# The first unit's query, key scores and routing made head by head, with the order of the gathered rows unchanged

## The chip, the cores and the metric

The kernel runs on one core of one Trainium2 chip. The metric is the time of one execution in microseconds (us), measured on the device. Lower is better.

## What is computed

The reference is two transformer blocks over 256 tokens of width 1024. The change lies in the expert layer of the first block (`peer_ffn`), which picks 16 of 16,384 experts for each of 8 heads and each token, and needs one row of `u` and one of `v` for each:

```python
def token_block(xt):                       # 128 tokens
    q = (xt @ wq).reshape(128, 8, 2, 128)
    s = jnp.einsum('thcd,hckd->thck', q, sub_keys)
    top_s, top_i = lax.top_k(s, 16)        # per head, for each of two key sets
    cand = top_s[:, :, 0, :, None] + top_s[:, :, 1, None, :]
    best_s, best_c = lax.top_k(cand.reshape(128, 8, 256), 16)
    i1 = jnp.take_along_axis(top_i[:, :, 0], best_c // 16, axis=-1)
    i2 = jnp.take_along_axis(top_i[:, :, 1], best_c % 16, axis=-1)
    expert = i1 * 128 + i2
    w = jax.nn.softmax(best_s, axis=-1)
    act = jax.nn.gelu(jnp.einsum('thkd,td->thk', u[expert], xt))
    return jnp.einsum('thk,thkd->td', w * act, v[expert])
```

Before it come a norm, the mixers and the output projection `w_out`; behind it a gate (`ple`) and the whole second block.

## The kernel before, in words

Each engine runs its own program, written out in order; the engines meet through counting semaphores (`wait_ge`, `then_inc`). Nothing reorders the work: whatever stands behind a waiting instruction on its engine waits too.

The tokens are two tiles of 128. A *unit* is one tile and one pair of heads (`HPAIR` = 2), so there are 8 units: 0 to 3 for tile 0, 4 to 7 for tile 1. A unit needs 32 gathered *rows* of `u` and 32 of `v` (`UROWS`); each is one indirect DMA of 128 x 1024 floats (0.52 MB), issued by POOL (`gather_u` L2603, `gather_v` L2616), with 8 slots for each side (`GATHER_SLOTS`). A row of `u` goes into a slot when DVE has used the one before it there (`u_used`). POOL first issues the 32 rows of unit 0, then waits for the key scores of all units (`sk_done`), and from then on alternates rows of `u` of the next unit and rows of `v` of this one.

For unit 0 the work goes through the engines thus. PE makes the query (`tile_query`, L973: four blocks of 128 columns, two for each head, 8 matmuls each, in one PSUM bank). ACT copies it (`query`, L1434). PE makes the scores (`key_scores`, L995). ACT copies them (`scores_out`, L1440). DVE searches the 16 best of each key set (`best_keys`, with helper `best16`), adds them in pairs and searches the 16 best sums (`best_sums`, L2165 to L2175), turns the places into expert numbers (`places`, `route`, L2195 to L2213, two operations on 128 x 1024 and a reduction of as much) and signals `idx_ready`. The four steps handle both heads of the unit; only the searches are called for each head.

PE's order around it is: turn tile 0, query 0 and scores 0 (unit 0), turn the mixer output of tile 1, output product of tile 1 (`tile_out(1)`, L959, two halves), query and scores of unit 1, turn tile 1, queries and scores of units 4 and 5, then those of the other four.

ACT's order is: the roots of tile 1's two mixer norms (L1279), which wait for DVE, then the copies of query 0 and scores 0, the token copy for DVE's products (L1447), and the copies of the turned tile 1 (L1416), on which the output product of tile 1 waits.

DVE's order is: key search, sums, places and routes of unit 0, residual of tile 1 (L1773), its mean, the first product of unit 0 (`products(0, 0, 1)`, L2220), the norm of tile 1 (L1785), key search and sums of unit 1, seven more products of unit 0, places and routes of unit 1, and the rest of unit 0's products.

SP loads the weights in chunks of 2 MB into a ring of three slots (L525); a chunk's load is issued when the chunk that held its slot is done (`chunk_done`). Chunk 1 of `peer_wq`, for the query of unit 1, waits for the first half of the output product of tile 1; chunk 2 for the second half; chunk 3 for the query of unit 4.

## Time and profile before

| | us |
|---|---|
| three runs | 1649.35, 1650.64, 1655.22 |
| the profiled execution | 1648.42 |
| its span in the profile | 1646.6 |
| PE busy in the span | 1429.4 |
| DVE busy | 972.0 |
| ACT busy | 537.5 |
| POOL busy | 510.8 |

The three runs have the median 1650.64. The span is what the profiler saw between the first and the last instruction; the execution's own time is 1.8 us more. Busy times are sums over the whole span; the engines work beside one another, and a matmul's row covers its way through a pipeline, so a busy PE is not a PE at its peak. A row of the timeline gives the start, the busy time, the operation, and in brackets how long the engine sat idle before it and what ended that.

### The profile page before, as it was taken

Reading aid. Unit: us, or ns where it says so; the run is one execution under the profiler, and the core shown is the slowest. Engines: PE = TensorE matmul, PEld = TensorE weight load, DVE = VectorE, ACT = ScalarE, POOL = GpSimd, SP = SyncE. Lnnn points to the kernel's source line nnn. Section 1 sums busy time; section 2 is a strip of 40 time slices with the busy share of each in tenths; the row PEclk is TensorE's granted clock in tenths of the full one; section 3 lists DMA queues with packets and bytes.
Section 4 is the critical chain, followed back from the end, with each engine's and each line's share of the span. In section 5 each row is a group of like instructions: output and inputs, shape, how many; then the busy total and the mean of one; then the engine's idle time right before and its main releaser. Section 6 shows DMA issues by size and latency. Waiting matters only on the chain. (4 is left out here: it accounts for less than half of the span.)

```text
span 1646.6 us, 17356 instructions
## 1 busy us (share of the span) xinstructions
PE 1429.4 (87%) x6624; PEld 943.0 (57%) x6624; DVE 972.0 (59%) x1758; ACT 537.5 (33%) x807; POOL 510.8 (31%) x550
## 2 busy tenths in 40 slices
PE   7999989677777777777777789999999989999998
PEld 6665667222222222222222466668998778689986
DVE  2255488566666667666545643565775365657763
ACT  3253321212121111111113245643443354434432
POOL 4000025767777777777676200000000000000000
PEclk9899999999999999999999999999999999999999
DMA  9323069999999999999999334224553545345543
GB/s 307 119 102 115 3 257 391 404 409 410 409 409 409 409 409 409 409 409 409 410 409 372 134 140 153 102 81 136 193 180 128 195 158 185 104 136 172 180 149 133
DMA packets 162578, 413.75 MB, mean 251 GB/s; under 512 B 11337, under 2 KB 57659, under 8 KB 162368
## 3 DMA queue, kind: packets, MB, share of 16 engines
q0 software_dynamic: 75632, 272.63, 42.1%
q1 hardware_dynamic: 86544, 138.58, 24.7%
q10 hardware_dynamic: 320, 1.43, 0.2%
q8 instruction: 53, 0.87, 0.2%
q14 instruction: 29, 0.24, 0.0%
HBM read 411.55 MB, written 1.05 MB: 251 GB/s over the span
## 5 line engine op out<-in xcount | busy, mean ns | idle before, releaser
L2220 DVE SCALAR_TENSOR_TENSOR arena<-arena,ps 128x1024 f32<-128x1024 f32 x256 | 309.3, 1220 | 224.0 <-DMA arena<-in_peer_u,routes 222.9
L2603 POOL DMA_INDIRECT arena<-in_peer_u,routes x256 | 241.8, 945 | 139.1 <-issue 63.2
L1813 DVE TENSOR_TENSOR w_lo<-ring,w_hi 128x2048 fp32r<-128x2048 f32 x66 | 151.1, 2292 | 103.3 <-ACT w_hi L1653 103.3
L1548 ACT ACTIVATE state<-cst,gatew 128x128 f32<-128x128 f32 x240 | 90.6, 397 | 342.9 <-PE ps L1047 342.8
L1653 ACT ACTIVATE w_hi<-ring 128x2048 fp32r<-128x2048 f32 x66 | 126.3, 1916 | 180.2 <-PE ps L1187 88.3
L1047 PE MATMUL ps<-mixed,state 128*128 128x512 f32 x240 | 118.5, 617 | 39.8 <-ACT state L1548 35.5
L1047 PE MATMUL ps<-wX,state 128*128 128x512 f32 x240 | 117.3, 611 | 40.9 <-DMA wX<-in_peer_v,routes 21.1
L1047 PE MATMUL ps<-xT,state 128*128 128x512 f32 x240 | 117.3, 611 | 39.0 <-ACT state L1548 26.5
L1047 PE MATMUL ps<-proj,state 128*128 128x512 f32 x240 | 117.3, 611 | 37.7 <-DMA proj<-in_peer_v,routes 20.2
L1047 PEld LDWEIGHTS ps<-mixed,state 128*128 128x128 f32 x240 | 41.5, 192 | 116.7 <-ACT state L1548 72.9
L1047 PEld LDWEIGHTS ps<-wX,state 128*128 128x128 f32 x240 | 40.6, 189 | 117.6 <-issue 71.4
L1047 PEld LDWEIGHTS ps<-xT,state 128*128 128x128 f32 x240 | 40.6, 189 | 115.6 <-ACT state L1548 67.4
L1047 PEld LDWEIGHTS ps<-proj,state 128*128 128x128 f32 x240 | 40.6, 189 | 114.3 <-issue 72.2
L1187 PE MATMUL ps<-x_lo,w_hi 128*128 128x256 f32 x704 | 99.4, 284 | 3.8 <-DVE x_lo L2458 3.8
L1187 PE MATMUL ps<-x_hi,w_hi 128*128 128x256 f32 x704 | 100.3, 285 | 0.0
L1187 PE MATMUL ps<-x_hi,w_lo 128*128 128x256 f32 x704 | 99.6, 284 | 0.0
L1187 PEld LDWEIGHTS ps<-x_lo,w_hi 128*128 128x128 f32 x704 | 91.3, 193 | 4.2 <-DVE x_lo L2458 4.2
L1187 PEld LDWEIGHTS ps<-x_hi,w_hi 128*128 128x128 f32 x704 | 91.4, 193 | 0.6 <-DVE x_hi L1794 0.4
L1187 PEld LDWEIGHTS ps<-x_hi,w_lo 128*128 128x128 f32 x704 | 91.6, 193 | 0.0
L2616 POOL DMA_INDIRECT proj<-in_peer_v,routes x64 | 62.7, 980 | 22.1 <-issue 16.8
L2616 POOL DMA_INDIRECT xT<-in_peer_v,routes x64 | 62.2, 971 | 20.1 <-issue 17.7
L2616 POOL DMA_INDIRECT wX<-in_peer_v,routes x64 | 61.0, 953 | 22.2 <-issue 16.5
(449 smaller groups left out, 2323.5 us busy)
## 6 DMA issues: line engine op xcount, KB each, us to landing
ring<-in_ffn_w_up SPq DMA_DIRECT2D x22, 2048.0 KB, 8.7
ring<-in_ffn_w_down SPq DMA_DIRECT2D x22, 1024.0 KB, 4.8
ring<-in_even_w_in SPq DMA_DIRECT2D x7, 2048.0 KB, 7.7
ring<-in_w_in SPq DMA_DIRECT2D x6, 2048.0 KB, 11.5
ring<-in_odd_w_in SPq DMA_DIRECT2D x6, 2048.0 KB, 7.7
ring<-in_peer_wq SPq DMA_DIRECT2D x4, 2048.0 KB, 8.7
ring<-in_w_out SPq DMA_DIRECT2D x2, 2048.0 KB, 7.9
arena<-in_peer_u,routes POOLq DMA_INDIRECT x256, 12.6
```

The lines of the kernel that those rows point to most:

```text
L1047: last = mm(ps[:, 4 + 2 * (u // PAIR_UNITS) + half_, :], diags[n % DIAGS], v_slots[b % GATHER_SLOTS][:, 512 * half_:512 * half_ + 512], st ...
L1187: last = mm(o, w[:, k, f * P:(f + 1) * P], x_[:, k, :], start=(step == k == 0), stop=(step == 2 and k == KD - 1))
L1548: do(diags[n % DIAGS], ident, ACT.Copy, scale=gatew[:, u * UROWS + b:u * UROWS + b + 1]).then_inc(diag_ready, 1)
L1653: do(w_hi[j % 2][:], w, ACT.Copy).then_inc(hi_ready, 1)
L1813: v.tensor_tensor(w_lo[j % 2][:], w, w_hi[j % 2][:].bitcast(F32), ALU.subtract).then_inc(lo_ready, 1)
L2220: v.scalar_tensor_tensor(row, row, 1.0, token_tile(u // PAIR_UNITS), ALU.mult, ALU.mult, accum_out=dots[:, b:b + 1]).then_inc(u_used, 1)
L2603: pool.indirect_dma_start(arena[:, b % GATHER_SLOTS, :], None, a["peer_u"][0], route_of(u, b))\
L2616: pool.indirect_dma_start(v_slots[b % GATHER_SLOTS], None, a["peer_v"][0], route_of(u, b))\
```

## The change

Unit 0's chain is split by heads. PE writes head 0's query into bank 2 and head 1's into bank 3 and signals each (`first_query`); the scores of a head (`head_scores`) go into banks 4 and 5, and those of head 0 stand inside the query of head 1, after 20 of the 32 matmuls. ACT copies a head's query and a head's scores by turns. DVE's `places` and `route` take a range of heads and are called for each head of unit 0, so that `idx_ready` counts up after head 0 and again after head 1; POOL waits for the first before row 0 and for the second before row 16. The order of the rows is the same. All other waits on `q_done`, `q_read`, `sk_done`, `sk_read` and `idx_ready` count one more; of them the diff shows those of `key_scores` and `scores_out`.

```diff
@@ -403,6 +403,14 @@
         def unit_scores(u):
 
             return proj[:, 2048 + 512 * u:2048 + 512 * (u + 1)]
+
+        def scores_count(u):
+
+            return SK_ORDER.index(u) + 2
+
+        def routed(u):
+
+            return u + 2
 
         def scores_at(u):
 
@@ -962,13 +970,38 @@
                         if (c, k) in steps:
                             attention_step(steps[c, k])
 
+            def head_scores(hd):
+
+                pe.wait_ge(q_read, hd + 1)
+                pe.wait_ge(keysT_ready, 1)
+                q_ = grid(proj[:, 0:1024], 2 * HPAIR, T)
+                for hc in (2 * hd, 2 * hd + 1):
+                    last = mm(ps[:, 4 + hd, hc * P:(hc + 1) * P], q_[:, hc, 0:P], keysT[:, hc, :], start=True, stop=True)
+                last.then_inc(sk_done, 1)
+
+            def first_query():
+
+                i1 = CHUNK_AT["peer_wq"]
+                begin(i1)
+                for j in range(2 * HPAIR):
+                    for k in range(KD):
+                        if j == 0:
+                            tile_ready("peer", 0, k)
+                        last = mm(ps[:, 2 + j // 2, j * P:(j + 1) * P], product_slot(i1)[:, k, j * P:(j + 1) * P], xT[:, k, 0:P],
+                                  start=(k == 0), stop=(k == KD - 1))
+                        if j % 2 and k == KD - 1:
+                            last.then_inc(q_done, 1)
+                        if (j, k) == (2, KD // 2 - 1):
+                            head_scores(0)
+                head_scores(1)
+
             def tile_query(c, tt, bank):
 
                 i1 = CHUNK_AT["peer_wq"] + c
                 begin(i1)
                 for j in range(2 * HPAIR):
                     for k in range(KD):
-                        if (c, j) == (0, 0):
+                        if (c, j, tt) == (0, 0, 1):
                             tile_ready("peer", tt, k)
                         last = mm(ps[:, bank, j * P:(j + 1) * P], product_slot(i1)[:, k, j * P:(j + 1) * P], xT[:, k, tt * P:(tt + 1) * P],
                                   start=(k == 0), stop=(k == KD - 1))
@@ -987,9 +1020,8 @@
             def key_scores(u, n_read):
 
                 place_, c, tt = SK_ORDER.index(u), u % PAIR_UNITS, u // PAIR_UNITS
-                pe.wait_ge(q_read, n_read)
-                if place_ >= SCORE_BANKS:
-                    pe.wait_ge(sk_read, place_ - SCORE_BANKS + 1)
+                pe.wait_ge(q_read, n_read + 1)
+                pe.wait_ge(sk_read, max(place_, 2))
                 q_ = grid(proj[:, (c % 2) * 1024:(c % 2 + 1) * 1024], 2 * HPAIR, T)
                 for hc in range(2 * HPAIR):
                     last = mm(ps[:, 4 + place_ % SCORE_BANKS, hc * P:(hc + 1) * P], q_[:, hc, tt * P:(tt + 1) * P], keysT[:, 2 * HPAIR * c + hc, :],
@@ -1002,9 +1034,7 @@
             pe.wait_ge(res_added, 2)
             filler(2, 3)
             tile_turn("peer", 0)
-            tile_query(0, 0, 2)
-            pe.wait_ge(keysT_ready, 1)
-            key_scores(0, 1)
+            first_query()
             tile_turn("out1", 1)
             tile_out(1)
             tile_query(1, 0, 0)
...
@@ -1436,7 +1466,7 @@
             def scores_out(u):
 
                 place_ = SK_ORDER.index(u)
-                act.wait_ge(sk_done, place_ + 1)
+                act.wait_ge(sk_done, scores_count(u))
                 do(unit_scores(u), ps[:, 4 + place_ % SCORE_BANKS, :], ACT.Copy).then_inc(sk_read, 1)
 
             def token_copied(tt):
@@ -1491,8 +1521,16 @@
             tile_turn("peer", 0, (1,))
             root("hg1", HH)
             root("nsa_o1", NH)
-            query(0, ps[:, 2, :], slice(0, 1))
-            scores_out(0)
+            for hd in range(HPAIR):
+                act.wait_ge(q_done, hd + 1)
+                at = slice(2 * hd, 2 * hd + 2)
+                do(proj[:, 0:1024].rearrange("p (j t n) -> p j t n", j=2 * HPAIR, t=TT)[:, at, 0, :],
+                   grid(ps[:, 2 + hd, :], 2 * HPAIR, P)[:, at, :], ACT.Copy).then_inc(q_read, 1)
+                if hd == 0:
+                    act.wait_ge(sk_done, 1)
+                    do(unit_scores(0)[:, 0:T], ps[:, 4, 0:T], ACT.Copy).then_inc(sk_read, 1)
+            act.wait_ge(sk_done, 2)
+            do(unit_scores(0)[:, T:2 * T], ps[:, 5, T:2 * T], ACT.Copy).then_inc(sk_read, 1)
             token_copied(0)
             tile_turn("out1", 1, (0, 1))
             tile_square(1, 0)
...
@@ -2177,7 +2215,7 @@
 
             def best_keys(u, hd):
 
-                dve.wait_ge(sk_read, SK_ORDER.index(u) + 1)
+                dve.wait_ge(sk_read, scores_count(u) if u else hd + 1)
                 two = slice(2 * hd, 2 * hd + 2)
                 best16(grid(unit_scores(u), 2 * HPAIR, NK)[:, two], grid(rest, 2 * HPAIR, NK)[:, two], top_v[:, two], top_i.bitcast(U32)[:, two], 2)
                 v.tensor_copy(top_f[:, two], top_i.bitcast(U32)[:, two])
@@ -2189,28 +2227,34 @@
                 best16(grid(cand, HPAIR, TOPK * TOPK)[:, one], grid(rest, HPAIR, TOPK * TOPK)[:, one],
                        best_v[:, one], best_i.bitcast(U32)[:, one], 1)
 
-            def places(u):
-
-                bi = small[:, 192 + UROWS:192 + 2 * UROWS].bitcast(U32)
-                v.tensor_scalar(halves[0].bitcast(U32), bi, 4, None, ALU.logical_shift_right)
-                v.tensor_scalar(halves[1].bitcast(U32), bi, 15, None, ALU.bitwise_and)
-                logits = grid(gatew[:, u * UROWS:(u + 1) * UROWS], HPAIR, TOPK)
-                link(v.tensor_tensor(logits, best_v, best_v[:, :, 0:1].broadcast_to((P, HPAIR, TOPK)), ALU.subtract))
+            def places(u, heads=slice(0, HPAIR)):
+
+                lo, n = heads.start, heads.stop - heads.start
+                at = slice(lo * TOPK, heads.stop * TOPK)
+                bi = small[:, 192 + UROWS:192 + 2 * UROWS].bitcast(U32)[:, at]
+                v.tensor_scalar(halves[0].bitcast(U32)[:, at], bi, 4, None, ALU.logical_shift_right)
+                v.tensor_scalar(halves[1].bitcast(U32)[:, at], bi, 15, None, ALU.bitwise_and)
+                logits = grid(gatew[:, u * UROWS:(u + 1) * UROWS], HPAIR, TOPK)[:, heads]
+                link(v.tensor_tensor(logits, best_v[:, heads], best_v[:, heads, 0:1].broadcast_to((P, n, TOPK)), ALU.subtract))
                 place4 = place.rearrange("p (h c k) -> p h c k", h=HPAIR, c=2)
                 for side in range(2):
-                    ins = v.tensor_copy(place4[:, :, side, :], grid(halves[side].bitcast(U32), HPAIR, TOPK))
+                    ins = v.tensor_copy(place4[:, heads, side, :], grid(halves[side].bitcast(U32), HPAIR, TOPK)[:, heads])
                 link(ins)
-                link(v.tensor_tensor(grid(onehot, 2 * UROWS, TOPK), cview("iota").unsqueeze(1).broadcast_to((P, 2 * UROWS, TOPK)),
-                                     over(place, (P, 2 * UROWS, TOPK)), ALU.is_equal))
-
-            def route(u):
-
-                hot = onehot.rearrange("p (h k j) -> p h k j", h=2 * HPAIR, k=TOPK)
-                link(v.tensor_tensor(hot, hot, top_f.unsqueeze(2).broadcast_to((P, 2 * HPAIR, TOPK, TOPK)), ALU.mult))
-                link(v.tensor_reduce(pick, grid(onehot, 2 * UROWS, TOPK), X, ALU.add))
-                pick4 = pick.rearrange("p (h c k) -> p h c k", h=HPAIR, c=2)
-                link(v.scalar_tensor_tensor(grid(halves[2], HPAIR, TOPK), pick4[:, :, 0, :], float(NK), pick4[:, :, 1, :], ALU.mult, ALU.add))
-                v.tensor_copy(routes[:, u * UROWS:(u + 1) * UROWS], halves[2]).then_inc(idx_ready, 1)
+                hot = grid(onehot, 2 * UROWS, TOPK)[:, 2 * TOPK * lo:2 * TOPK * heads.stop]
+                link(v.tensor_tensor(hot, cview("iota").unsqueeze(1).broadcast_to((P, 2 * TOPK * n, TOPK)),
+                                     over(place[:, 2 * TOPK * lo:2 * TOPK * heads.stop], (P, 2 * TOPK * n, TOPK)), ALU.is_equal))
+
+            def route(u, heads=slice(0, HPAIR)):
+
+                lo, n = heads.start, heads.stop - heads.start
+                at = slice(lo * TOPK, heads.stop * TOPK)
+                sides, both = slice(2 * lo, 2 * heads.stop), slice(2 * TOPK * lo, 2 * TOPK * heads.stop)
+                hot = onehot.rearrange("p (h k j) -> p h k j", h=2 * HPAIR, k=TOPK)[:, sides]
+                link(v.tensor_tensor(hot, hot, top_f[:, sides].unsqueeze(2).broadcast_to((P, 2 * n, TOPK, TOPK)), ALU.mult))
+                link(v.tensor_reduce(pick[:, both], grid(onehot, 2 * UROWS, TOPK)[:, both], X, ALU.add))
+                pick4 = pick.rearrange("p (h c k) -> p h c k", h=HPAIR, c=2)[:, heads]
+                link(v.scalar_tensor_tensor(grid(halves[2], HPAIR, TOPK)[:, heads], pick4[:, :, 0, :], float(NK), pick4[:, :, 1, :], ALU.mult, ALU.add))
+                v.tensor_copy(routes[:, u * UROWS:(u + 1) * UROWS][:, at], halves[2][:, at]).then_inc(idx_ready, 1)
 
             def products(u, lo, n):
 
@@ -2266,10 +2310,9 @@
             gate = MIX_AT[CHUNK_AT["ple_gate_w"], 0]
             for hd in range(HPAIR):
                 best_keys(0, hd)
-            for hd in range(HPAIR):
                 best_sums(hd)
-            places(0)
-            route(0)
+                places(0, slice(hd, hd + 1))
+                route(0, slice(hd, hd + 1))
             tile_residual(1)
             tile_mean(1)
             dve.wait_ge(token_ready, 1)
@@ -2616,13 +2659,14 @@
                 pool.indirect_dma_start(v_slots[b % GATHER_SLOTS], None, a["peer_v"][0], route_of(u, b))\
                     .then_inc(v_landed[b % GATHER_SLOTS], 16)
 
-            pool.wait_ge(idx_ready, 1)
             for b in range(UROWS):
+                if b % TOPK == 0:
+                    pool.wait_ge(idx_ready, b // TOPK + 1)
                 gather_u(0, b)
-            pool.wait_ge(sk_done, UNITS)
+            pool.wait_ge(sk_done, UNITS + 1)
             for u in range(UNITS):
                 if u + 1 < UNITS:
-                    pool.wait_ge(idx_ready, u + 2)
+                    pool.wait_ge(idx_ready, routed(u + 1))
                 for b in range(UROWS):
                     if u + 1 < UNITS:
                         gather_u(u + 1, b)
```

PE, from the turn of tile 0 on (`ps<-xT,ring` is the query, `ps<-wX,proj` the scores, `ps<-cst,mixed` the turn of the mixer output of tile 1), before:

```order
L973 MATMUL ps<-xT,ring 128x128 [waits xT_low,chunk_loaded0]
L973 MATMUL ps<-xT,ring 128x128 x3
L973 MATMUL ps<-xT,ring 128x128 [waits xT_high]
L973 MATMUL ps<-xT,ring 128x128 x27
L995 MATMUL ps<-wX,proj 128x128 [waits q_read,keysT_ready]
L995 MATMUL ps<-wX,proj 128x128 x3
L557 MATMUL ps<-cst,mixed 128x128 [waits tile_src]
```

and in the change:

```order
L990 MATMUL ps<-xT,ring 128x128 [waits xT_low,chunk_loaded0]
L990 MATMUL ps<-xT,ring 128x128 x3
L990 MATMUL ps<-xT,ring 128x128 [waits xT_high]
L990 MATMUL ps<-xT,ring 128x128 x15
L979 MATMUL ps<-wX,proj 128x128 [waits keysT_ready,q_read]
L979 MATMUL ps<-wX,proj 128x128
L990 MATMUL ps<-xT,ring 128x128 x12
L979 MATMUL ps<-wX,proj 128x128 [waits keysT_ready,q_read]
L979 MATMUL ps<-wX,proj 128x128
L565 MATMUL ps<-cst,mixed 128x128 [waits tile_src]
```

Two of the four score matmuls, with their wait for ACT's copy of head 0 (`q_read`), have moved ahead of the last twelve matmuls of the query.

ACT, from the two roots of tile 1's norms (`std<-var`) to the token copy (`ps<-hn`), before:

```order
L1279 ACTIVATE std<-var 128x4 [waits var_ready]
L1279 ACTIVATE std<-var 128x8 [waits var_ready]
L1434 ACTIVATE proj<-ps 128x4x128 [waits q_done]
L1440 ACTIVATE proj<-ps 128x512 [waits sk_done]
L1447 ACTIVATE ps<-hn 128x1024 [waits tile_src]
```

and in the change:

```order
L1309 ACTIVATE std<-var 128x4 [waits var_ready]
L1309 ACTIVATE std<-var 128x8 [waits var_ready]
L1527 ACTIVATE proj<-ps 128x2x128 [waits q_done]
L1531 ACTIVATE proj<-ps 128x256 [waits sk_done]
L1527 ACTIVATE proj<-ps 128x2x128 [waits q_done]
L1533 ACTIVATE proj<-ps 128x256 [waits sk_done]
L1477 ACTIVATE ps<-hn 128x1024 [waits tile_src]
```

The two copies have become four of half the size, behind the same root; the token copy stands behind all four.

DVE, from the end of the second head's sums in unit 0 to the residual of tile 1, before:

```order
L2175 MAX_INDEX k2tok<-k2tok,state 128x8 [waits dve_chain]
L2195 TENSOR_SCALAR k2tok<-k2tok 128x32 [waits dve_chain]
L2196 TENSOR_SCALAR k2tok<-k2tok 128x32
L2198 TENSOR_TENSOR gatew<-k2tok 128x32
L2201 CAST k2tok<-k2tok 128x2x16 [waits dve_chain]
L2201 CAST k2tok<-k2tok 128x2x16
L2203 TENSOR_TENSOR state<-cst,k2tok 128x1024 [waits dve_chain]
L2209 TENSOR_TENSOR state<-state,k2tok 128x1024 [waits dve_chain]
L2210 TENSOR_REDUCE k2tok<-state 128x64 [waits dve_chain]
L2212 SCALAR_TENSOR_TENSOR k2tok<-k2tok 128x32 [waits dve_chain]
L2213 CAST routes<-k2tok 128x32 [waits dve_chain]
L1773 TENSOR_TENSOR h<-h,ps 128x512 [waits chunk_done] x2
```

and in the change, from the end of the first head's sums to the key search of the second head (the rows of `places` and `route` stand once more behind the second head's sums, ahead of the residual):

```order
L2213 MAX_INDEX k2tok<-k2tok,state 128x8 [waits dve_chain]
L2235 TENSOR_SCALAR k2tok<-k2tok 128x16 [waits dve_chain]
L2236 TENSOR_SCALAR k2tok<-k2tok 128x16
L2238 TENSOR_TENSOR gatew<-k2tok 128x16
L2241 CAST k2tok<-k2tok 128x16 [waits dve_chain]
L2241 CAST k2tok<-k2tok 128x16
L2244 TENSOR_TENSOR state<-cst,k2tok 128x512 [waits dve_chain]
L2253 TENSOR_TENSOR state<-state,k2tok 128x512 [waits dve_chain]
L2254 TENSOR_REDUCE k2tok<-state 128x32 [waits dve_chain]
L2256 SCALAR_TENSOR_TENSOR k2tok<-k2tok 128x16 [waits dve_chain]
L2257 CAST routes<-k2tok 128x16 [waits dve_chain]
L2203 MAX k2tok<-proj 128x8 [waits sk_read]
```

The ten operations of `places` and `route` are issued for each head at half the size, the first time ahead of the second head's key search.

## Rows read from the trace of the kernel before

**Rows 1.** the page: GB/s in the 40 slices of 41.2 us; queues: packets, MB, share

```profile
GB/s 307 119 102 115 3 257 391 404 409 410 409 409 409 409 409 409 409 409 409 410 409 372 134 140 153 102 81 136 193 180 128 195 158 185 104 136 172 180 149 133
...
q0 software_dynamic: 75632, 272.63, 42.1%
q1 hardware_dynamic: 86544, 138.58, 24.7%
```

**Rows 2.** timeline of POOL: start us, us, engine, line, operation [idle <-releaser]

```profile
221.84 1.03 POOL L2603 DMA_INDIRECT arena<-in_peer_u,routes  x1 [17.20 <-DVE routes L2213]
...
231.90 0.94 POOL L2603 DMA_INDIRECT arena<-in_peer_u,routes  x1 [0.30 <-issue]
245.27 0.93 POOL L2603 DMA_INDIRECT arena<-in_peer_u,routes  x1 [12.43 <-DVE arena L2220]
```

**Rows 3.** one window: length, busy PE, PEld, DVE, ACT, POOL; PEclk, DMA share, GB/s

```profile
241.00:242.00 1.00, 0.45 (x5) 0.26 (x3) 0.93 (x4) 0.51 (x1) 0.00 (x0) 1.00 0.00 0
```

**Rows 4.** timeline of PE, 190 to 232

```profile
194.51 7.38 PE L973 MATMUL ps<-xT,ring 128*128 128x128 f32 x64 [0.88 <-DVE xT L1762]
203.31 1.13 PE L995 MATMUL ps<-wX,proj 128*128 128x128 f32 x8 [1.42 <-ACT proj L1434]
...
207.19 13.97 PE L959 MATMUL ps<-ring,xT 128*128 128x512 f32 x32 [1.88 <-ACT xT L1416]
222.27 7.41 PE L973 MATMUL ps<-xT,ring 128*128 128x128 f32 x64 [1.11 <-DMA ring<-in_peer_wq]
230.37 1.16 PE L995 MATMUL ps<-wX,proj 128*128 128x128 f32 x8 [0.69 <-ACT proj L1434]
```

**Rows 5.** timeline of ACT, 202 to 206

```profile
202.47 0.21 ACT L1279 ACTIVATE std<-var 128x8 f32<-128x8 f32 x1 [6.35 <-DVE var L1888]
202.59 0.58 ACT L1434 ACTIVATE proj<-ps 128x512 f32<-128x512 f32 x1
...
204.97 1.02 ACT L1447 ACTIVATE ps<-hn 128x1024 f32<-128x1024 f32 x1
```

**Rows 6.** timeline of DVE, 205 to 233

```profile
205.11 0.49 DVE L2165 MAX8 k2tok<-proj 128x8 f32<-128x128 f32 x2 [1.47 <-ACT proj L1440]
...
208.07 0.42 DVE L2184 TENSOR_TENSOR state<-k2tok 128x256 f32<-128x256 f32 x1
...
211.94 0.43 DVE L2165 MAX8 k2tok<-state 128x8 f32<-128x256 f32 x1
...
216.68 0.18 DVE L2195 TENSOR_SCALAR k2tok<-k2tok 128x32 uint32<-128x32 uint32 x1
...
217.38 1.23 DVE L2203 TENSOR_TENSOR state<-cst,k2tok 128x1024 f32<-128x1024 f32 x1
...
221.38 0.18 DVE L2213 CAST routes<-k2tok 128x32 uint32<-128x32 f32 x1
...
232.19 0.49 DVE L2165 MAX8 k2tok<-proj 128x8 f32<-128x128 f32 x2 [0.23 <-ACT proj L1440]
```

**Rows 7.** two gaps of PE, after each a window with its granted clock

```profile
298.08 1.19 PE L1047 MATMUL ps<-mixed,state 128*128 128x512 f32 x1 [3.52 <-ACT state L1548]
301.00:302.00 1.00, 1.00 (x3) 0.44 (x3) 0.00 (x0) 0.97 (x3) 0.69 (x2) 0.89 1.03 401
...
965.13 3.65 PE L545 MATMUL ps<-cst,hn 128*128 128x128 f32 x16 [5.37 <-ACT hn L1274]
970.00:971.00 1.00, 1.00 (x6) 0.79 (x5) 1.00 (x4) 0.00 (x0) 0.00 (x0) 0.89 0.00 0
```

**Rows 8.** loads of `peer_wq`, chunks 1 and 2: each one's issue and time to landing

```profile
L525 SPq DMA_DIRECT2D ring<-in_peer_wq x1: 368/368/368, 214.3 to 214.3; - x1
...
DMA to landing us min/median/max: 7.9/7.9/7.9
...
L525 SPq DMA_DIRECT2D ring<-in_peer_wq x1: 368/368/368, 221.2 to 221.2; - x1
...
DMA to landing us min/median/max: 11.8/11.8/11.8
```

6 lines of the change are left out of this document (3 added, 3 removed).

## The prediction

> **What bounds the kernel now.** I read the page first: its moved bytes by slice stand at 409 GB/s from slice 9 to slice 21, some 500 us in which the DMA engines never rest [rows 1]. This is the stage in which 512 gathers of 0.52 MB fetch the expert rows. In it nothing but the transfers counts; the time at which this full stream begins sets its end, and all later work follows it. So the question is when the stream begins.
>
> The timeline of POOL answers it. Row 0 of the first unit is issued at 221.84, row 8 at 231.90, and then POOL waits 12.43 us for DVE [rows 2]: eight slots are full and DVE must use one. Row 9 goes out at 245.27, and from there on the stream is full. Just before, the DMA engines move nothing at all [rows 3]. The start of the full stream is therefore row 9, not row 0. Row 9 needs the second product of unit 0 on DVE, and in DVE's program that stands behind the key search of unit 1 (`best_keys(1)`, `best_sums`), which begins at 232.19 after a wait of only 0.23 us for ACT's copy of unit 1's scores [rows 6]. On PE those scores come at 230.37, behind the query product of unit 1, which starts at 222.27 after 1.11 us of waiting for the second chunk of `peer_wq` [rows 4]. This is the path: chunk 1 of `peer_wq`, query 1, scores 1, key search 1, row 9.
>
> **The change part by part.** *PE.* The query of unit 0 is 32 matmuls, 64 records, from 194.51 in 7.38 us [rows 4]. After 20 of them (40 records, 4.61 us), at 199.12, PE now stops for ACT's copy of head 0. ACT can't give it: in its own order the roots of tile 1's norms come first, and the last, for which it waits 6.35 us on DVE, runs at 202.47; before, the copy began at 202.59 [rows 5]. A copy of 128x512 takes 0.58 and one of 128x1024 1.02, so 128x256 takes about 0.36 on their line: done at 202.95, and PE resumes 0.14 later (as 203.17 to 203.31 before), at 203.10. Before, PE had used these 4 us to finish the product. Now follow half the scores (0.57 of 1.13), the 24 records left (2.77), the wait for the second copy (0.05 + 0.36 + 0.14) and the other scores (0.57): end at 207.6, before at 204.44, so 3.1 us late.
>
> *Clock.* PE is idle for 3.98 us. The nearest gap in the trace is 3.52 us, after which PE restarts at 298.08 at a granted clock of 0.5 and has 1.00 again soon after 301, which is 3 us of work at the lower of its two levels (1.2 for 2.4 GHz), or 1.5 us lost [rows 7]. The other end is zero: after the gaps of 1.42 and 1.88 us [rows 4] nothing was lost. Upwards, the gap of 5.37 us before 965.13 was followed by the low level until nearly 971, 2.9 us lost [rows 7]. I take 1.3, near the 3.52 us gap and a little less, since the gap is longer and more of the low stretch then falls in it. PE is 4.4 us late after the scores. ACT's last copy is 0.2 shorter, so the output product of tile 1 begins 4.2 late (207.19 to 211.4) and ends 4.2 late.
>
> *DVE and the first rows.* Head 0's scores are on hand at 203.10 + 0.57 + 0.5 (clock) + 0.41 (copy) = 204.6, not at 205.11. A head costs 3.42 for its keys (205.11 to 211.94 is two), 2.37 for its sums (211.94 to 216.68 is two), and for places and routes 4.88 (216.68 to 221.56) less what halving saves [rows 6]. Three of those operations fall from 1024 to 512 elements: 1.23 at 1024 and 0.42 at 256 put 512 at 0.69, so 3 x 0.54 = 1.62 goes and 3.26 stays; the other seven are nearly all fixed cost and are now issued twice. One head is 9.05 us. Routes of head 0 are ready at 213.65, and POOL's row 0 goes out at 213.9, **7.9 us earlier**. Head 1 is ready at 222.7, 1.1 later than before; that is covered, as DVE's next work, the residual of tile 1, now waits for PE until 225.4, and row 16 is far off. Row 8 now needs DVE's first product, behind that residual and its norm; it is one row in an empty stretch and costs nothing.
>
> *What the early rows meet.* The load of `peer_wq` chunk 1 is released by the first half of the output product, at 214.33, and lands 7.9 us later in an empty stretch. The next chunk, issued at 221.2 together with the first rows, took 11.8 [rows 8]. In the changed order chunk 1 is issued at 214.33 + 4.2 = 218.5, into rows 0 to 7 (4.2 MB, which at 409 GB/s are 10.3 us of transfer begun only at about 216). It stands where chunk 2 stood, so I take 11.8: landed at 230.3. The lower end is 7.9; the upper is all of it at once, 6.3 MB in 15.4 us behind 213.9 and a latency of 2.8 (7.9 less 2.1 MB at 409 GB/s), 232.1.
>
> The Trainium skill ("DMA: Bandwidth & Descriptors", section "Queues, rings and completion order") says that each DMA engine takes turns between its queues packet by packet. By that rule rows whose packets are 3.6 KB on average would get more than twice the share of weights with 1.6 KB packets [rows 1], the chunk would land with the last of the rows at about 232.1, and the sum would be 1.8 us higher. The 11.8 us of chunk 2 speak for about equal shares: 2.1 MB in some 9 to 10 us.
>
> *Query 1.* It starts at 230.4 rather than 222.27, **8.1 late**. PE has then been idle for 5.0 us (225.4 to 230.4); between 0 and 2.9 us as above, I take 0.8, less than at the first place because the gap is longer. Scores 1, and with them the key search of unit 1 on DVE, come 8.9 us late: DVE is waiting for them and has no slack to give, as it waited before too. Row 9 is issued at 254.2. Everything from there on (chunk 3, the other queries, POOL's wait for the last scores) keeps its distance, and the stream has the same bytes left.
>
> **Sum.** 4.2 (stop, clock, shorter copy) + 3.9 (11.8 - 7.9) + 0.8 = 8.9 us, with the first 7.9 us of earlier gathers worth nothing. The profiled execution took 1648.42 us (span 1646.6 and 1.8 around it), the runs 1649.35, 1650.64 and 1655.22; the middle of these four is 1650.0, which I use as the base. Forecast 1658.9, 0.54% slower. A measurement of this kernel tells about 0.5%, 8.25 us, from no change, so the forecast lies just over the edge.
>
> **The rivals.**
> 1. *The load is not held up by the rows.* PE's stop alone remains: chunk 1 lands at 218.5 + 7.9 = 226.4, 4.2 late, and the second clock gap is gone. 1654.2; without the first clock loss 1652.9. For it: chunk 1 has a head start on half of the rows' bytes that chunk 2 did not have. Against it: 11.8 in rows 8.
> 2. *The load comes last and the clock stays low.* It lands at 232.1, and each gap costs 2.9: 9.9 + 2.9 = 12.8, so 1662.8. For it: the 965 us gap, and the skill's rule of turns. Against it: chunk 2.
> 3. *The early rows shorten the stream.* If the stream's end is set by how many rows are out, and DVE reaches its second product early, the 7.9 us come back whole: 1642.1. It decides at one point: the key search of unit 1 would have to begin no later than 224.3 (232.19 - 7.9). Query 1 has to end first, and its weights had landed only at 222.2 before. I see no way.
> 4. *The change does not bite:* ACT reaches the copy by 199.1, nothing stops, head 0 is merely early. 1650.0. Against it: the 6.35 us wait on DVE ahead of ACT's copy, which nothing in the change moves.
>
> **Chances.** Forecast 0.55, rival 1 0.22, rival 2 0.13, rival 3 0.04, rival 4 0.06. The forecast stands near the edge, so I give 0.34 of its 0.55 to slower by over 0.5%; with rival 2 that is 0.47. Within 0.5% are the rest of it (0.21), rivals 1 and 4 and half of rival 3, 0.51. Faster is 0.02. The range goes from 1652, under rival 1, to 1664, over rival 2; outside remain rivals 3 and 4 and what I have not thought of.
>
> **What would show it.** In the new profile: a PE gap of about 4 us inside the query product of unit 0, ended by ACT; POOL's row 0 near 213.9; chunk 1 of `peer_wq` issued near 218.5 with a landing near 11.8; PE waiting for it about 5 us; the granted clock at 0.5 twice; POOL's wait before row 9 grown from 12.4 us to over 20 and row 9 near 254.2, with a hole in the DMA rates before it of over 10 us. A landing of 8 us would prove rival 1, row 9 before 245 would prove the whole path wrong.

## The result and the profile after

The changed kernel took 1666.59 us (median of 4 runs, 1664.99 to 1668.54), beside 1650.82 of the kernel before (4 runs, 1649.35 to 1655.22). The ratio is 1.0103, with a 95% interval of 1.0089 to 1.0117: **slower by 1.0%**, or some 16 to 17 us, where the prediction said 8.9 (0.54%) and ended its range at 1664. The direction and the path were those of the forecast, and the size was not: it is outside the range.

The page of the profiled execution (its own time 1664.99) shows the same picture as [rows 1], with the sixth and seventh slices of the rates lower (219 and 280 GB/s, where 257 and 391 stood). PE is busy 12 us longer for the same 6624 instructions (1441.4 us, 1429.4 before). The rates by slice:

```profile
GB/s 297 125 101 114 3 219 280 402 409 409 409 409 409 409 410 409 410 409 410 409 409 370 205 124 158 118 63 145 195 169 144 168 163 181 118 128 181 178 148 131
```

One thing has to be taken out before the two traces are laid side by side. The first query starts at 196.78, and in [rows 4] it starts at 194.51. These 2.27 us arise in the first 25 us of the program, in code that the change does not touch; the last section shows it. Times "on the clock of before" below are those of the trace less 2.27.

POOL, the rows that answer to [rows 2]:

```profile
216.21 1.03 POOL L2646 DMA_INDIRECT arena<-in_peer_u,routes  x1 [9.30 <-DVE routes L2257]
...
225.39 0.94 POOL L2646 DMA_INDIRECT arena<-in_peer_u,routes  x1 [0.30 <-issue]
232.14 1.94 POOL L2646 DMA_INDIRECT arena<-in_peer_u,routes  x1 [5.82 <-DVE arena L2264]
262.26 0.93 POOL L2646 DMA_INDIRECT arena<-in_peer_u,routes  x1 [28.18 <-DVE arena L2264]
```

Row 0 goes out at 216.21, on the clock of before 213.94, 7.9 us earlier, as forecast. Row 8 waits 5.8 us for DVE's first product. Then POOL waits **28.18 us** before row 9, where it waited 12.43. Row 9 stands at 260.0 on the clock of before, 14.7 late; forecast were 8.9.

PE, the rows that answer to [rows 4]:

```profile
196.78 4.70 PE L990 MATMUL ps<-xT,ring 128*128 128x128 f32 x40 [0.87 <-DVE xT L1800]
205.27 1.22 PE L979 MATMUL ps<-wX,proj 128*128 128x128 f32 x4 [3.79 <-ACT proj L1527]
206.28 5.07 PE L990 MATMUL ps<-xT,ring 128*128 128x128 f32 x24
211.83 0.71 PE L979 MATMUL ps<-wX,proj 128*128 128x128 f32 x4 [0.47 <-ACT proj L1527]
...
215.08 13.97 PE L967 MATMUL ps<-ring,xT 128*128 128x512 f32 x32 [1.67 <-ACT xT L1446]
237.09 9.58 PE L1006 MATMUL ps<-xT,ring 128*128 128x128 f32 x64 [8.04 <-DMA ring<-in_peer_wq]
```

ACT, the rows that answer to [rows 5]:

```profile
204.74 0.21 ACT L1309 ACTIVATE std<-var 128x8 f32<-128x8 f32 x1 [6.35 <-DVE var L1926]
204.85 0.37 ACT L1527 ACTIVATE proj<-ps 128x256 f32<-128x256 f32 x1
```

The query is cut after 40 records (the trace has two records for each matmul of the query). The stop of 3.79 us is there, ended by ACT's copy, which stands behind the root that waits 6.35 us for DVE. Behind the stop the four records of scores take 1.22 us and the other 24 of the query 5.07, where half of the whole had been 0.57 and 24 records 2.77. The output product starts at 215.08 (212.8 on the clock of before, 5.6 late, not 4.2). Then PE waits 8.04 us for the second chunk of `peer_wq`, and the query behind it takes 9.58 instead of 7.41.

The granted clock (third figure from the end) and the moved bytes (last) in windows of 1 us; the length comes first, then busy PE, PEld, DVE, ACT and POOL:

```profile
204.00:205.00 1.00, 0.00 (x0) 0.00 (x0) 0.69 (x3) 0.26 (x2) 0.00 (x0) 0.56 0.00 0
210.00:211.00 1.00, 1.00 (x7) 1.00 (x7) 0.93 (x4) 0.00 (x0) 0.00 (x0) 0.53 0.00 0
231.00:232.00 1.00, 0.00 (x0) 0.00 (x0) 0.96 (x4) 1.00 (x1) 0.00 (x0) 0.71 1.04 408
241.00:242.00 1.00, 1.00 (x8) 1.00 (x8) 0.00 (x0) 0.00 (x0) 0.00 (x0) 0.67 1.06 389
248.00:249.00 1.00, 1.00 (x11) 1.00 (x10) 0.00 (x0) 0.45 (x1) 0.00 (x0) 1.00 0.00 0
```

Twice the clock is at its lower level (0.50, that is 1.2 GHz). The means of the windows put the first time from 204.1, in the stop, to 210.9, which is 5.7 us beyond the stop, and the second from 231.4, in the wait for the load, to 241.7, which is 4.6 us beyond that wait. At 248 nothing is moved: the hole before row 9, 2 us long before [rows 3], now lasts from 243 to 259.

SP's load of chunk 1 (issue, then time to landing), which answers to the first load of [rows 8]:

```profile
L533 SPq DMA_DIRECT2D ring<-in_peer_wq x1: 367/367/367, 222.2 to 222.2; - x1
...
DMA to landing us min/median/max: 14.8/14.8/14.8
```

It is issued at 222.2 (219.9 on the clock of before, 5.6 late) and lands **14.8 us** later. Before it was 7.9, and I had taken 11.8.

DVE, at head 0's keys and at the key search of unit 1 [rows 6]:

```profile
206.94 0.49 DVE L2203 MAX8 k2tok<-proj 128x8 f32<-128x128 f32 x2 [1.04 <-ACT proj L1531]
...
249.18 0.49 DVE L2203 MAX8 k2tok<-proj 128x8 f32<-128x128 f32 x2 [15.91 <-ACT proj L1470]
```

Head 1's key search follows at 215.84, so one head costs 215.84 - 206.94 = 8.90 (forecast 9.05). The first search starts 0.44 earlier than before on the same clock, as forecast. DVE then stands idle for 15.91 us ahead of unit 1's search. Rows 1 to 7 have landed by 235.5 and wait in their slots for products that stand behind that search.

The delay of row 9 goes through to the end of the stream. Its last gather, before and then after:

```profile
916.12 0.93 POOL L2616 DMA_INDIRECT proj<-in_peer_v,routes  x1 [0.30 <-issue]
...
933.43 0.94 POOL L2659 DMA_INDIRECT proj<-in_peer_v,routes  x1 [0.30 <-issue]
```

It is 15.0 us late on the clock of before, and the two profiled executions (1648.42 and 1664.99) differ by 14.3 once the 2.27 are taken out.

### The profile page after: what moved, and what is told of

It reads as the page before. It is cut to its first block and busy times, and to the rows that moved or that the text cites. A ratio compares the mean times of both kernels' runs of the same rounds, so it can differ in the third digit from the quotient of the medians.

```text
span 1663.2 us, 17370 instructions
## 1 busy us (share of the span) xinstructions
PE 1441.4 (87%) x6624; PEld 950.4 (57%) x6624; DVE 973.3 (59%) x1768; ACT 537.8 (32%) x809; POOL 512.6 (31%) x550
## 5 line engine op out<-in xcount | busy, mean ns | idle before, releaser
L1077 PEld LDWEIGHTS ps<-wX,state 128*128 128x128 f32 x240 | 41.2, 191 | 116.7 <-issue 66.3
## 6 DMA issues: line engine op xcount, KB each, us to landing
arena<-in_peer_u,routes POOLq DMA_INDIRECT x256, 12.5
```

What stands on the lines that cost most here:

```text
L1077: last = mm(ps[:, 4 + 2 * (u // PAIR_UNITS) + half_, :], diags[n % DIAGS], v_slots[b % GATHER_SLOTS][:, 512 * half_:512 * half_ + 512], st ...
```

## The experiments

Theory A was: two causes that add up, PE's stop inside the query (with its clock loss), and the early rows, which hold up the load on which the query of unit 1 waits. Rival B gave everything to the stop, rival C everything to the rows.

### No stop: first the whole query, then the scores

```diff
-                        if (j, k) == (2, KD // 2 - 1):
-                            head_scores(0)
-                head_scores(1)
+                for hd in range(HPAIR):
+                    head_scores(hd)
```

(ACT copies both heads' queries, then both heads' scores.)

> The change, but PE makes the whole query of unit 0 first and then both heads' scores, so it does not stop inside the query; the rows of head 0 still go out early. Theory A (two causes: PE's stop, and the early rows holding up the load of peer_wq chunk 1): the load is issued near 214 again but meets rows 0 to 7 and lands some 13 to 15 us later, near 228 to 229; PE waits for it about 7 us and loses about 2 us to the clock; the kernel is 6 to 9 us slower than before, so 1657 to 1660, and 7 to 9 faster than the change. Rival B (PE's stop does all the damage, rows are harmless): the load lands within 10 us, the time is within 2 us of before, 1649 to 1653. Rival C (the early rows do it all): as slow as the change, 1666.

Measured: 1658.78 us beside 1650.54, ratio 1.0053 (1.0036 to 1.0069). PE's timeline at the two queries:

```profile
196.72 7.38 PE L990 MATMUL ps<-xT,ring 128*128 128x128 f32 x64 [0.88 <-DVE xT L1797]
...
230.34 9.50 PE L1005 MATMUL ps<-xT,ring 128*128 128x128 f32 x64 [7.45 <-DMA ring<-in_peer_wq]
```

POOL's timeline at row 9:

```profile
255.43 0.94 POOL L2643 DMA_INDIRECT arena<-in_peer_u,routes  x1 [25.57 <-DVE arena L2261]
```

The load of chunk 1, issue and time to landing:

```profile
L533 SPq DMA_DIRECT2D ring<-in_peer_wq x1: 368/368/368, 216.1 to 216.1; - x1
...
DMA to landing us min/median/max: 14.2/14.2/14.2
```

The query is whole again, 7.38. The load is issued where it was before (216.1, less 2.2 of this execution's late start), and lands 14.2 us later; PE waits 7.45, and the query of unit 1 takes 9.50 after it. Half of the loss is here without any stop. B and C both fall. In this run only row 0 was issued ahead of the load (215.65, 0.45 us earlier), and the DMA engines were not slow while it was under way (rate last):

```profile
220.00:225.00 5.00, 2.89 (x7) 0.95 (x5) 4.69 (x16) 0.03 (x1) 3.77 (x5) 1.00 1.04 411
```

Rows 1 and 3, issued behind the load (issue, then time to landing):

```profile
L2643 POOL DMA_INDIRECT arena<-in_peer_u,routes x1: 982/982/982, 217.0 to 217.0; - x1
...
DMA to landing us min/median/max: 7.7/7.7/7.7
...
L2643 POOL DMA_INDIRECT arena<-in_peer_u,routes x1: 941/941/941, 219.5 to 219.5; - x1
...
DMA to landing us min/median/max: 9.3/9.3/9.3
```

They landed at 224.7 and 228.8, with row 2 between them, all three ahead of the load (230.3). What is issued behind a load counts here, not only what stands ahead of it. The rows land 2.05 us apart while the load is under way, and in that time some 0.82 MB move (400 GB/s); a row is 0.52 of it, so by my estimate the rows get 1.8 bytes for each of the load's, and the load some 145 GB/s.

### The stop alone: no row before both heads' routes

```diff
             for b in range(UROWS):
-                if b % TOPK == 0:
-                    pool.wait_ge(idx_ready, b // TOPK + 1)
+                if b == 0:
+                    pool.wait_ge(idx_ready, 2)
```

> The change, but POOL issues no row before the routes of both heads are ready; PE's stop stays. Theory A: the load is issued near 220 to 222, lands 8 to 9 us later, PE waits for it at most 2 us; row 0 goes out near 225; what is left is the stop with its clock loss, 3.1 + 3.0 us: 6 to 7 us slower than before, 1656 to 1658. Rival B: all of the loss stays, 1664 to 1667. Rival C: no loss, 1650 to 1652.

Measured: 1657.53, ratio 1.0053 (1.0033 to 1.0072). PE's timeline, at the rest of the first query and at the query of unit 1:

```profile
205.97 4.92 PE L990 MATMUL ps<-xT,ring 128*128 128x128 f32 x24
...
229.61 7.41 PE L1006 MATMUL ps<-xT,ring 128*128 128x128 f32 x64 [1.02 <-DMA ring<-in_peer_wq]
```

POOL's timeline at row 9:

```profile
252.61 0.94 POOL L2646 DMA_INDIRECT arena<-in_peer_u,routes  x1 [15.75 <-DVE arena L2264]
```

The load of chunk 1:

```profile
L533 SPq DMA_DIRECT2D ring<-in_peer_wq x1: 368/368/368, 221.8 to 221.8; - x1
...
DMA to landing us min/median/max: 7.8/7.8/7.8
```

The load is issued as late as in the change, at 221.8, and lands in 7.8 us, because row 0 now leaves 3 us behind it. PE waits 1.02 and the query takes 7.41. What is left is the stop: 24 records in 4.92 us, and row 9 is 5.4 late. Theory A expected 6 to 7 us; the ratio says 8.7, with 5.4 to 11.9 in its interval.

### Neither

Both edits together.

> Both undone: no stop, no early rows; what is left of the change is the split of copies on ACT and of places and routes on DVE. Theory A and both rivals: within 2 us of before, 1649 to 1653. If it is slower by more, the split itself costs something that I have not counted.

Measured: 1650.07, ratio 0.9998 (0.9984 to 1.0012; 10 runs). Row 9 stands at 247.41, less 2.1 that is 245.3, where [rows 2] have it. The split of the copies and of `places` and `route` costs nothing that can be measured, and gains nothing by itself. Its trace also shows the clock fall without a long gap. PE's timeline at the query of unit 4, which took 7.46 us before:

```profile
236.89 9.52 PE L1005 MATMUL ps<-xT,ring 128*128 128x128 f32 x64 [0.47 <-ACT xT L1445]
```

PE had been busy for 0.50 to 0.66 of each window of 1 us from 231 to 235, with no listed wait above 0.97 us, and the granted clock went to 0.50 all the same, from about 234 to 241. POOL's row behind the last scores came 2.8 us later than before.

### The clock: matmuls in the two gaps

```diff
                         if (j, k) == (2, KD // 2 - 1):
+                            filler(4, 4)
                             head_scores(0)
...
             tile_out(1)
+            filler(0, 8)
             tile_query(1, 0, 0)
```

`filler(bank, n)` makes n matmuls of 128x512 whose result nobody reads.

> The change, with matmuls whose result nobody reads in PE's two gaps: four of 128x512 before head 0's scores, eight before the query of unit 1. They fit in the gaps (3.8 and 8.0 us at 0.93 each). Theory A with the clock as a third part: the granted clock stays at 1.00, the first half of the stage gains 3.0 us and the query of unit 1 2.2 us, so 4.5 to 5.5 us faster than the change, 1661 to 1662. Rival (the clock loss is covered by the load, which lands when the rows are through): only the 2.2 us of the query come back, 1664.

Measured: 1659.59, ratio 1.0067 (1.0046 to 1.0087), 6 us under the change by the two ratios. PE's timeline, at head 0's scores, the rest of the query, and the query of unit 1:

```profile
203.09 0.71 PE L979 MATMUL ps<-wX,proj 128*128 128x128 f32 x4 [0.36 <-ACT proj L1529]
203.64 2.84 PE L990 MATMUL ps<-xT,ring 128*128 128x128 f32 x24
...
233.81 7.41 PE L1007 MATMUL ps<-xT,ring 128*128 128x128 f32 x64 [2.76 <-DMA ring<-in_peer_wq]
```

The load of chunk 1:

```profile
L533 SPq DMA_DIRECT2D ring<-in_peer_wq x1: 368/368/368, 217.3 to 217.3; - x1
...
DMA to landing us min/median/max: 16.4/16.4/16.4
```

Scores 0.71, rest of the query 2.84, query of unit 1 7.41: the clock loss is gone at both places. This execution has no late start (first query at 194.59). The load is issued at 217.3, 2.6 earlier than in the change, and lands at 233.7, only 1 earlier than 234.7. So the clock loss at the first place is mostly covered by the wait for the load, as the rival said; the time, however, gained 6 and not 2 us. The trace of this one execution accounts for 3.3 of that at row 9 (256.7 against 260.0); the two intervals together leave some 2 to 10 us open for the difference, so the rival's 2 us isn't excluded by the times alone.

### Four early rows

```diff
             for b in range(UROWS):
-                if b % TOPK == 0:
-                    pool.wait_ge(idx_ready, b // TOPK + 1)
+                if b in (0, 4):
+                    pool.wait_ge(idx_ready, b // 4 + 1)
```

> The change, but only rows 0 to 3 go out after head 0; rows 4 to 31 wait for head 1. Theory A (the load lands late because the bytes of the rows issued before and with it go through first): four rows are nearly through when the load is issued, it lands 8 to 10 us after its issue, and the time is near that of the version with late rows, 0.4 to 0.6% slower than before. Rival E (any row beside the load holds it up, or the load's own late place does): it lands 13 us or more after its issue and the time stays 0.8 to 1.1% slower than before.

Measured: 1662.88, ratio 1.0083 (1.0046 to 1.0120). PE's timeline at the query of unit 1:

```profile
233.85 8.92 PE L1006 MATMUL ps<-xT,ring 128*128 128x128 f32 x64 [5.74 <-DMA ring<-in_peer_wq]
```

POOL's timeline at rows 4 and 9:

```profile
224.47 0.93 POOL L2646 DMA_INDIRECT arena<-in_peer_u,routes  x1 [4.16 <-DVE routes L2257]
...
258.37 0.94 POOL L2646 DMA_INDIRECT arena<-in_peer_u,routes  x1 [25.23 <-DVE arena L2264]
```

The load of chunk 1:

```profile
L533 SPq DMA_DIRECT2D ring<-in_peer_wq x1: 368/368/368, 221.3 to 221.3; - x1
...
DMA to landing us min/median/max: 12.5/12.5/12.5
```

The landing time is 12.5 us, between the two expectations and nearer the rival's. The time, 0.83% slower, lies in the rival's range, though its interval reaches into that of theory A. The four rows were issued at 215.5 to 219.4 and landed in 4.4 to 6.0, so the last was through at 225.4, 4 us after the load's issue; rows 4 to 7 left from 224.47, just as in the version with late rows, where the load took 7.8. Rows 1 to 3 were still under way at the issue (they landed at 222.0, 223.8 and 225.4), at most 1.6 MB, or 3.8 us at 409 GB/s, and the load took 4.7 us more than without them. That the bytes ahead of the load count fits this; that they are all of it does not, and the run without the stop showed the same from the other side.

### Would early rows pay if row 9 were free?

The forecast put the start of the stream at row 9, held by DVE's order. Four versions take the products of rows 1 to 13 between the parts of unit 1's search:

```diff
             tile_norm(1)
-            for hd in range(HPAIR):
-                best_keys(1, hd)
-            for hd in range(HPAIR):
-                best_sums(hd)
-            products(0, 1, 7)
-            places(1)
-            route(1)
-            products(0, 8, 12)
+            products(0, 1, 3)
+            best_keys(1, 0)
+            products(0, 4, 2)
+            best_keys(1, 1)
+            products(0, 6, 2)
+            best_sums(0)
+            products(0, 8, 2)
+            best_sums(1)
+            products(0, 10, 2)
+            places(1)
+            products(0, 12, 2)
+            route(1)
+            products(0, 14, 6)
```

Two of them also issue eight rows of unit 1 ahead of POOL's wait for the last scores:

```diff
-            pool.wait_ge(sk_done, UNITS + 1)
+            pool.wait_ge(idx_ready, routed(1))
+            for b in range(GATHER_SLOTS):
+                gather_u(1, b)
+            pool.wait_ge(sk_done, UNITS + 1)
```

(with three of every four later steps of unit 0 issuing the remaining rows of unit 1).

> The version without PE's stop and with early rows, and two things more: DVE uses rows 1 to 13 of unit 0 between the parts of unit 1's search instead of behind it, so POOL's row 9 no longer waits for the query of unit 1; and POOL issues eight rows of unit 1 ahead of its wait for the last scores. Theory A (the stream of gathers starts at row 9; what starts it earlier counts in full as long as rows are there to issue): row 9 goes out before 235, the hole in the DMA rates before 255 closes, the time is 3 to 8 us under before, 1643 to 1648. Rival D (the wait for the last scores is the true start of the stream, and the late load still delays those scores by 8 us): the hole moves to the time before the last scores and the time stays 4 to 8 us above before.

> As the one before, but row 0 waits for both heads. The load of chunk 1 lands in 8 us again. Theory A: only the hole of 2.5 us near 241 closes, 1 to 3 us under before, 1647 to 1650. Rival D: within 1 us of before, as the last scores come at the same time.

> The version without PE's stop and with early rows, and DVE's new order alone; POOL waits for the last scores as in the change. Theory A: row 9 before 235, but all 32 rows are then out some 10 us before the last scores, and the DMA engines run dry there: 0 to 5 us above before, 1651 to 1656. Rival (row 9 never mattered): as slow as the version without the stop, 1657 to 1660.

> The kernel before with DVE's new order alone. Theory A: row 9 goes out near 233 and not at 245, the hole near 241 closes, and what is left in flight at the last scores covers it: 0 to 3 us under before. Rival (row 9 never mattered): within 0.5 us.

All four ran on a chip on which the kernel before takes 1728.6 us, and came out, in this order, at 0.9875 (0.9848 to 0.9902), 0.9903 (0.9879 to 0.9927), 0.9909 (0.9885 to 0.9933) and 0.9904 (0.9878 to 0.9930) of it. The kernel before and the change were then run beside two of them on the same slow chip:

> The kernel before, unchanged, so that its trace and its times stand beside those of the other three on one chip. All theories: equal to before within 0.2%.

> The change, unchanged, on the same chip as the others. Theory A: 0.8 to 1.2% slower than before, with the load of chunk 1 landing 14 to 16 us after its issue; on a chip with slower gathers the loss can be smaller, as the stream then waits for other things too.

> The kernel before with DVE's new order alone, again, as the first comparison of it ran on a chip on which before took 1728 us. Theory A: on a chip where before takes 1650, 0 to 3 us under before; the 14 us gained in the first comparison belong to the other chip. Rival (they belong to the order): again 0.9 to 1% faster.

> No stop, early rows, DVE's new order, eight rows of unit 1 ahead of the wait for the last scores, again. Theory A: 3 to 8 us under before. Rival D (the last scores are the true start): 0 to 8 us above.

The kernel before stood at 1.0000 (0.9987 to 1.0014), the change at 1.0038 (1.0021 to 1.0055), the order alone at 0.9911 (0.9878 to 0.9944), all early at 0.9883 (0.9861 to 0.9906). The change lost 0.4% and not the 0.8 to 1.2% expected, though PE waited 7.95 us for chunk 1 there too. The waits of the kernel before on this chip (engine and line, what for: us in total, times, longest) show something that the trace of [rows 1] does not have at all:

```profile
ACT state L1548 <- remote: 210.7, 50, 10.8
...
ACT proj L1434 <- remote: 42.6, 3, 23.1
```

ACT stands still for up to 10.8 and 23.1 us at a time for something that the profile books as "remote", outside the recorded engines. In the gather stage the rates are 320 to 395 GB/s by slice instead of 409. Which of it is the chip's and which the order's can't be told there, so three of the versions ran again on a chip with 1649.32 for the kernel before:

> The kernel before with DVE's new order alone, a third time, for a chip on which before takes about 1650. Theory A: row 9 goes out some 10 us earlier than before and closes the hole near 241; 0 to 3 us under before. Rival: 0.9 to 1% faster, as on the chip with 1730.

> No stop, early rows, DVE's new order, eight rows of unit 1 ahead, for a chip on which before takes about 1650. Theory A: 3 to 8 us under before. Rival D (the last scores are the true start and come 8 us late): 0 to 8 us above.

> As the one before, but with late rows, on the same chip. Theory A: 1 to 3 us under before.

| version | us | ratio to before (95%) |
|---|---|---|
| before, DVE's new order | 1646.46 | 0.9982 (0.9965 to 0.9998) |
| all early | 1653.72 | 1.0020 (1.0004 to 1.0036) |
| all late | 1649.11 | 0.9993 (0.9976 to 1.0010) |

The version with early rows, the new order and POOL's old wait was not run on this chip. Only the first of the three beats the kernel before, by 0.2%, and it has late rows. All early came out 3 us above, in rival D's range and not in theory A's. POOL's timeline in the first, at row 9 and at the first row behind the wait for the last scores:

```profile
235.35 0.94 POOL L2608 DMA_INDIRECT arena<-in_peer_u,routes  x1 [0.48 <-DVE arena L2220]
...
288.51 0.94 POOL L2608 DMA_INDIRECT arena<-in_peer_u,routes  x1 [8.34 <-DVE arena L2220]
```

A window of 5 us of the same kernel, the moved bytes last:

```profile
265.00:270.00 5.00, 3.89 (x22) 3.17 (x21) 4.93 (x10) 1.02 (x1) 2.27 (x3) 1.00 0.71 210
```

Row 9 leaves at 235.35, which is 233.3 less this execution's late start of 2.0, and 11.9 us earlier than before. The waits that stood before row 9 are now small pieces of 0.5 to 4 us, and the rates stay near 400 up to 260. But the rows run out before the last scores are there: POOL waits 8.34 us, where the kernel before waited 8.28 for those scores (the row names DVE as the one that came last), and the rates drop to 210 GB/s at 265. Twelve us won at row 9 are worth 3 us at the end. Theory A was right that row 9 holds the stream back, and rival D was right that the last scores do too, close behind it. With early rows the load delays those scores as well. PE's timeline of the version with all early, at the query of unit 1:

```profile
232.85 9.29 PE L1005 MATMUL ps<-xT,ring 128*128 128x128 f32 x64 [7.40 <-DMA ring<-in_peer_wq]
```

And its load of chunk 1:

```profile
L533 SPq DMA_DIRECT2D ring<-in_peer_wq x1: 368/368/368, 218.6 to 218.6; - x1
...
DMA to landing us min/median/max: 14.2/14.2/14.2
```

The load lands 14.2 us after its issue, PE waits 7.40 and loses the clock. Early rows cost some 0.3% even where everything else is arranged for them (1.0020 against 0.9993; the two intervals overlap a little).

## Why the prediction was wrong in size

**The path was right, and each link of it is in the trace.** The early rows left 7.9 us earlier and were worth nothing; PE stopped where it should, ended by ACT behind the root that waits for DVE; the load of chunk 1 went late into the rows; the query, the scores and the search of unit 1 came late; row 9 with them. The version with neither cause is equal to before (0.9998).

**Three terms of the sum were too small**, on the clock of before:

| term | forecast | measured |
|---|---|---|
| stop, first clock loss, shorter copy | 4.2 | 5.6 (output product 207.19 to 212.8) |
| load, landing time over 7.9 | 3.9 | 6.9 (14.8) |
| second clock loss | 0.8 | 2.2 (9.58 - 7.41) |
| row 9 | 8.9 | 14.7 |

The three measured terms add up to the 14.7 at row 9.

**The landing time.** The step that failed most is "It stands where chunk 2 stood, so I take 11.8": the load took 14.8 us. It does not stand there. Chunk 2 was issued 0.6 us ahead of row 0; chunk 1 in the change is issued 6.0 us behind it, with rows 0 to 4 out. How much the place matters is in the other traces, where the same 2 MB meet the first rows:

| load | issued, from row 0 | landing, us |
|---|---|---|
| chunk 1, late rows | 3.0 ahead | 7.8 |
| chunk 2, neither | 1.7 ahead | 9.8 |
| chunk 2, before | 0.6 ahead | 11.8 |
| chunk 1, no stop | 0.4 behind | 14.2 |
| chunk 1, fillers | 3.8 behind | 16.4 |
| chunk 1, the change | 6.0 behind | 14.8 |

Over 3.4 us of place the landing time goes from 7.8 to 14.2, so chunk 2 was a sample from the middle of a steep slope. The rows ahead of the load are not the reason on that slope, as there is at most one. The rows issued behind it are, as the run without the stop shows: they leave the load some 145 GB/s, at which its 2.1 MB would take 14.5 us.

I had also named 13.6 us as the upper end (232.1 for a load at 218.5), with the argument that nothing can land later than the eight rows and the load moved at 409 GB/s. The load landed at 234.7 on the clock of before, 2.6 later. The windows of 1 us up to that landing add up to 6.7 MB, where I had counted 6.3: at least 0.4 MB of row 8 (issued at 232.14) or chunk 2 (229.1) went through ahead of its end, by my estimate 0.9 us at 409 GB/s. The rest is the rate, which stood at 262 to 373 GB/s from 219 to 227.

The trace agrees with what the Trainium skill says ("DMA: Bandwidth & Descriptors", section "Queues, rings and completion order"), that each DMA engine takes turns between queues packet by packet: rows 5 to 7 were issued behind the load (222.55 to 225.39) and landed ahead of it (231.4, 233.4 and 235.5; the load at 237.0). I had set this rule aside on the strength of chunk 2, and it was the better guide to the order in which things land. The share that I had drawn from the packet sizes, more than two to one for the rows, was nearer than the equal shares that I read out of chunk 2: the estimate from the run without the stop is 1.8 to one. Chunk 2 itself shows as much in the trace of before: beside it rows 0 and 1 landed 2.0 us apart (229.2 and 231.3), and once it was in (233.0) rows 3 and 4 landed 1.3 apart (235.2 and 236.5). It took only 11.8 us because it had a start on the rows.

**The clock.** I took 1.3 and 0.8 us from a gap of 3.52 us, arguing that after a longer gap more of the low stretch lies inside the gap. The losses were 3.0 (0.65 in the scores and 2.3 in the query, against a whole of 0.57 and 2.77) and 2.2 us. The argument was wrong: the low level lasted 5.7 and 4.6 us into the work behind the gaps, against 3.1 behind the gap of 3.52 us. The gap of 5.37 us in [rows 7] cost 2.9, and I had used it as a bound only. Nor do the losses go by the length of the gap: 3.0 us behind 3.79, 1.5 behind 5.74 (four early rows: 8.92 - 7.41), 2.2 behind 8.04, and 2.1 behind waits of under 1 us (neither: 9.52 - 7.46). Fillers in the gaps removed both losses. The first loss was 1.65 us more than forecast, of which 1.4 reached the output product, and part of that vanished in the wait for the load.

**The sum at row 9 and the time.** In the single changes row 9 was late by 8.0 (no stop; measured 0.53%, 8.7 us), 5.4 (late rows; 0.53%, 8.7 us), 11.5 (four early rows; 0.83%, 13.7 us) and 0.0 (neither; 0.02%). By the medians 0.7 to 3.3 us more are lost than that, in the change too (14.7 of 16 to 17). The traces show no such rest in the stream: its last gather is late by 8.2, 5.1 and 10.7 us in the first three and by 15.0 in the change, each less its late start. A profiled execution is one of the several behind a median, so the rest can be scatter; it isn't explained further. The two causes alone give 8.0 + 5.4 = 13.4 at row 9, and together 14.7: they nearly add up.

**The range** ended at 1664 because I combined the bad ends only in rival 2 and gave them 0.13. The measured case is rival 2 in kind (load last, clock low at both places) and 2 us beyond it at row 9. Two of the three terms came out at or above the upper ends that I had named (2.9 for the first clock loss, 13.6 for the landing), the third below its own (2.9). Rival 3 is refuted by the 28.18 us before row 9, rival 4 by the stop of 3.79 us, rival 1 by the landing time.

## What to carry to other kernels

Starting transfers earlier gains nothing if the limit on slots stops them anyway, and it can cost: here eight early rows nearly doubled the landing time (7.8 or 7.9 us to 14.8) of the one weight load that the next unit waited for. Before a step is split so that its first half is ready sooner, look at which engine has to answer in the middle of it and whether that engine is free at that time; PE stopped for 3.8 us because ACT stood behind a root that waited for DVE. For a load that enters among others, count what is issued behind it while it is under way as well as what stands ahead, and don't take its landing time from a load that stood 1 us or more elsewhere. For a new gap of TensorE, take the clock loss as a range from all the gaps of the trace; the length of the gap alone did not tell it here.

## What the runs showed beside that

**The first product of the program has two lengths.** PE's row of the first weight chunk, in the timeline of before:

```profile
15.21 7.17 PE L926 MATMUL ps<-xT,ring 128*128 128x256 f32 x32 [1.16 <-DMA ring<-in_w_in]
```

and after:

```profile
15.31 9.38 PE L934 MATMUL ps<-xT,ring 128*128 128x256 f32 x32 [1.26 <-DMA ring<-in_w_in]
```

The same 32 records take 7.17 or 9.38 us, at a granted clock of 1.00 in both, and everything behind moves by 2.2. The change itself took 7.17 in its profile on the slow chip, so this varies from one execution to another with the same kernel. The version with neither cause has 9.21 and equals before in the median. Two single profiles can differ by 2 us for it alone; what makes it was not tried.

**The first rows moved at about 300 GB/s in the change, and not in every version.** Its rates are 262 to 352 GB/s from 220 to 227, with only rows 0 to 7 and, from 222 on, the load under way, though POOL issued one row of 0.52 MB each 1.24 us, which would be 422 GB/s. With four early rows it is 281 to 340 from 218 to 225. Without the stop, where the load was there from the start, it is 393 to 420 from 219 to 227. In the full stream the same rows reach 409. What makes the difference was not tried.

**A chip on which the same kernel takes 1730 us** had ACT held up 50 times for 210.7 us in all at the one line L1548. On it the change costs 0.4% instead of 1.0%, and DVE's new order gains 0.9% instead of 0.2%. A ratio from one chip is not that of another.
